# Two regions instead of three for the dense weights of a hybrid decoder trunk, and an early load of the third expert pair's down weights

## What is computed

```python
h = x @ w_in                                   # (256,1024) @ (1024,2048)
u, q, k, v, qm = jnp.split(h, list(SPLITS), axis=-1)
q, k = partial_rotary(heads(q), cos, sin), partial_rotary(heads(k), cos, sin)
y_pool = multiscale_pool(u, w_pool, pool_scale)
y_dsa = dilated_attention(q, k, heads(v))      # 8 heads x 64
km, vm = jnp.split(mem @ w_mem_kv, 2, axis=-1)
y_mem = memory_attention(heads(qm), heads(km), heads(vm))   # 4 heads x 64
mix = jnp.concatenate([y_pool, y_dsa, y_mem], axis=-1) @ w_out
x = layer_norm(DEEPNORM_ALPHA * x + mix, ln1_g, ln1_b)
# 64 routed experts of width 256, top 8 of them for each token, and one shared expert
top_idx, top_w = route(x, w_router, router_bias)
ffn = routed_experts(x, top_idx, top_w, w_gate, w_up, w_down) + swiglu(x, ws_gate, ws_up, ws_down)
x = layer_norm(DEEPNORM_ALPHA * x + ffn, ln2_g, ln2_b)
```

## Time and profile before

| | |
|---|---|
| median of 3 runs | 1214.82 us (1214.5 to 1215.64) |
| the profiled execution, by its own time | 1215.07 us |
| its span, first to last instruction | 1213.0 us |
| TensorE busy | 1180.3 us, 97% of the span |
| read from HBM | 450.15 MB |
| DMA over the span | 373 GB/s |
| dense part of layer 0, then its loop | up to 156.19 us, then to about 601 us |
| dense part of layer 1, then its loop | up to 752.81 us, then to 1199.5 us |

### The profile page before, as it was taken

One profiled execution on the slowest core, in us unless ns is written; L12 is line 12 of the kernel. 1 busy time (PEld: TensorE's weight loads), 2 busy tenths in 40 slices (PEclk: granted clock), 3 DMA queues, 4 the chain that ended last, 5 costly groups with the idle time before them and its releaser, 6 DMA issues.

```text
span 1213.0 us, 17943 instructions
## 1 busy us (share of the span) xinstructions
PE 1180.3 (97%) x7776; PEld 560.9 (46%) x7776; DVE 351.0 (29%) x1071; ACT 263.0 (22%) x513; POOL 10.4 (1%) x20
## 2 busy tenths in 40 slices
PE   7999999999999999999899999999999999999994
PEld 6774544444444444444386645444444444444431
DVE  0433722222222222222334246222222222222224
ACT  1132322112222122221112313222212222112210
POOL 0000000000000000000000000000000000000001
PEclk9999999999999999999999999999999999999998
DMA  9972399999999999999997406999999999999992
GB/s 385 424 317 73 119 408 427 429 425 427 428 425 428 427 427 428 427 426 426 421 388 306 182 35 242 405 427 427 427 426 428 426 427 428 427 427 427 427 426 111
DMA packets 36070, 452.45 MB, mean 373 GB/s; under 512 B 3984, under 2 KB 4112, under 8 KB 6928
## 3 DMA queue, kind: packets, MB, share of 16 engines
q1 hardware_dynamic: 35984, 451.22, 88.5%
HBM read 450.15 MB, written 1.05 MB: 372 GB/s over the span
## 4 chain that ended last, share of the span: by engine, by line
PE 90%; DMA 7%; DVE 2%; ACT 1%; issue 0%; POOL 0%; POOLq 0%; DVEq 0%
PE bank L620 34%; PE bank L646 17%; PE bank L540 8%; DMA slots<-in_w_gu 7%; PE bank L565 5%; PE bank L719 5%; PE bank L791 4%; PE bank L728 2%; PE bank L632 2%; PE bank L917 1%; PE bank L738 1%; PE bank L748 1%; PE bank L587 1%; PE bank L552 1%; PE bank L824 1%; PE bank L674 1%
## 5 line engine op out<-in xcount | busy, mean ns | idle before, releaser
L646 PE MATMUL bank<-slots,low 128*32 128x512 f32 x2048 | 233.0, 595 | 2.3 <-issue 2.3
L620 PE MATMUL bank<-slots,low 128*64 128x512 f32 x1024 | 226.9, 594 | 3.6 <-DMA slots<-in_w_gu 3.5
L620 PE MATMUL bank<-slots,xT 128*64 128x512 f32 x1024 | 226.3, 594 | 1.3 <-ACT xT L956 1.0
L1238 DVE SCALAR_TENSOR_TENSOR yparts<-bank,small,yparts 128x512 fp32r<-128x512 f32 x128 | 96.1, 751 | 249.1 <-ACT yparts L956 249.1
L540 PEld LDWEIGHTS bank<-high,low 128*128 128x128 bf16 x1536 | 108.2, 147 | 50.3 <-issue 49.7
L620 PEld LDWEIGHTS bank<-slots,low 128*64 128x64 f32 x1024 | 69.0, 137 | 134.3 <-issue 127.0
L620 PEld LDWEIGHTS bank<-slots,xT 128*64 128x64 f32 x1024 | 69.2, 137 | 131.1 <-issue 128.1
L1230 DVE TENSOR_TENSOR high<-high,bank 128x256 f32<-128x256 f32 x64 | 27.0, 421 | 329.7 <-ACT high L978 329.7
L956 ACT ACTIVATE yparts<-bank,small 128x512 fp32r<-128x512 f32 x128 | 88.1, 688 | 157.9 <-PE bank L646 157.9
L540 PE MATMUL bank<-high,low 128*128 128x128 bf16 x1536 | 117.7, 227 | 0.2
L646 PEld LDWEIGHTS bank<-slots,low 128*32 128x32 f32 x2048 | 60.7, 109 | 121.1 <-issue 117.2
(11 more groups left out here) (129 smaller groups left out, 667.4 us busy)
## 6 DMA issues: line engine op xcount, KB each, us to landing
slots<-in_w_gu SPq DMA_DIRECT2D x128, 2048.0 KB, 24.6
slots<-in_w_dn SPq DMA_DIRECT2D x64, 2048.0 KB, 24.4
slots<-in_dense SPq DMA_DIRECT2D x30, 1024.0 KB, 15.2
slots<-in_first SPq DMA_DIRECT2D x4, 768.0 KB, 7.7
r<-in_pool_mat SPq DMA_DIRECT2D x2, 1024.0 KB, 23.9
r<-in_ln_g SPq DMA_DIRECT2D x4, 512.0 KB, 4.8
r<-in_ln_b SPq DMA_DIRECT2D x4, 512.0 KB, 5.9
slots<-in_shared_dn SPq DMA_DIRECT2D x2, 1024.0 KB, 5.0
```

The costliest lines, as they stand in the source:

```text
L620: m = pe.matmul(H[64 * a:64 * a + 64, :], xg[B % 2][:, k, j, a, :], GU[g][:, a, :, k, :], start=k == 0, stop=k == KD - 1)
L646: m = pe.matmul(Y[half][r0:r0 + 32, :], hT[:, kc * P + 64 * a + 32 * t:kc * P + 64 * a + 32 * t + 32], DN[g][:, a, kc, half * 512:(half + ...
L1238: dve.scalar_tensor_tensor(ysp[:, 1, half * 512:(half + 1) * 512], Y[half][:, :], wslot[:, b:b + 1], ysp[:, 0, half * 512:(half + 1) * 512 ...
```

## The change

The dense blocks rotate through regions 0 and 1 alone: block c goes to region c % 2, and its load waits for the last use of block c - 2 rather than c - 3. Region 2, the DN of slot 2, is no longer used by dense weights, and the down weights of pair 2 are loaded into it early: in layer 0 behind pair 1's weights, in layer 1 at the head of the layer, once pair 29 has used its own. The GU of pair 2 is loaded in the other order: its second half (region 1) after sh1, its first half (region 0) after acc3. The small loads (tokens, router and small weights, pooling matrix) change their place in SyncE's order, and layer 0's pair 0 goes from ahead of them to behind blocks 3 and 4. Pair 1's weights stand behind block 5 as they did, but block 5 waited for raw3 and now waits for v1. `shared_up` of the first token tile waits for the two halves of its block apart.

```diff
--- before.py
+++ after.py
@@ -407,9 +407,9 @@
 
             def chunk(l, c):
 
-                r = c % 3
-                if c > 3 or c == 3 and l:
-                    sp.wait_ge(*full_at(l, LAST_USE[c - 3]))
+                r = c % 2
+                if c >= 3 or c == 2 and l:
+                    sp.wait_ge(*full_at(l, LAST_USE[c - 2]))
                 name = CHUNKS[c]
                 if name == "sd":
                     sp.dma_start(region[r][:, 0:KF * D], shared_dn[l]).then_inc(chunk_in[r][0], 16)
@@ -471,36 +471,42 @@
                 if l == 0:
                     sp.dma_start(cst[:], consts).then_inc(const_in, 16)
                     sp.dma_start(bo[:], before_ones).then_inc(const_in, 16)
+                    chunk(l, 2)
+                    sp.dma_start(xs[:], x[0].rearrange("(t p) d -> p t d", p=P)).then_inc(x_in, 16)
+                    sp.dma_start(sw[:], small_w[l]).then_inc(small_in, 16)
+                    sp.dma_start(r8[:], pool_mat).then_inc(pool_in, 16)
+                    chunk(l, 3)
+                    chunk(l, 4)
+                    load_gu(main, l, 0, 0)
+                    load_dn(main, l, 0, 0)
                 else:
                     sp.wait_ge(main.y_full, 2 * last + 2)
-                chunk(l, 2)
-                if l == 0:
+                    load_dn(main, l, 2, 2)
+                    sp.wait_ge(main.y_full, 2 * (l * PAIRS - 1))
+                    load_gu(main, l, 0, 0)
+                    load_dn(main, l, 0, 0)
+                    chunk(l, 2)
+                    sp.wait_ge(*x_before(l))
+                    sp.dma_start(sw[:], small_w[l]).then_inc(small_in, 16)
+                    sp.dma_start(r8[:], pool_mat).then_inc(pool_in, 16)
                     chunk(l, 3)
-                if l:
-                    sp.wait_ge(main.y_full, 2 * (l * PAIRS - 1))
-                load_gu(main, l, 0, 0)
-                load_dn(main, l, 0, 0)
-                if l == 0:
-                    sp.dma_start(xs[:], x[0].rearrange("(t p) d -> p t d", p=P)).then_inc(x_in, 16)
-                else:
-                    sp.wait_ge(*x_before(l))
-                sp.dma_start(sw[:], small_w[l]).then_inc(small_in, 16)
-                sp.dma_start(r8[:], pool_mat).then_inc(pool_in, 16)
-                for c in range(3 if l else 4, 6):
-                    chunk(l, c)
+                    chunk(l, 4)
+                chunk(l, 5)
                 load_gu(main, l, 1, 1)
                 load_dn(main, l, 1, 1)
+                if l == 0:
+                    load_dn(main, l, 2, 2)
                 chunk(l, 6)
-                chunk(l, 7)
                 sp.wait_ge(*full_at(l, "pooled"))
                 norms(l, ln1_g, ln1_b)
+                chunk(l, 7)
                 chunk(l, 8)
                 sp.wait_ge(*x_at(l, 0, NT - 1))
                 norms(l, ln2_g, ln2_b)
                 sp.wait_ge(*full_at(l, "sh1"))
-                load_gu(main, l, 2, 2)
+                load_gu(main, l, 2, 2, (1,))
                 sp.wait_ge(*full_at(l, "acc3"))
-                load_dn(main, l, 2, 2)
+                load_gu(main, l, 2, 2, (0,))
                 run(main, l, l, None)
                 with sp.If(count_in[sp.engine, l] > SLOTS):
                     rounds(sp, l, run)
@@ -529,7 +535,7 @@
             def chunk_wait(l, c, halves=(0, 1)):
 
                 for h in halves:
-                    pe.wait_ge(chunk_in[c % 3][h], 48 * l + 16 * (c // 3) + (16 if c % 3 else 0))
+                    pe.wait_ge(chunk_in[c % 2][h], 64 * l + 16 * (c // 2 + (c % 2 or l)))
 
             def gather(ps, B, quarter, buf, to=G):
 
@@ -580,7 +586,7 @@
                 pe.wait_ge(*read_at(l, f"shT{t}"))
                 if t == 0 and half == 1:
                     chunk_wait(l, 8)
-                wd = region[2][:, 0:KF * D].rearrange("p (k n) -> p k n", k=KF)
+                wd = region[0][:, 0:KF * D].rearrange("p (k n) -> p k n", k=KF)
                 name = f"acc{2 * t + half}"
                 o = fill(l, name)
                 for kc in range(KF):
@@ -716,7 +722,7 @@
                         for k in range(KD):
                             if i % 2 == 0 and j == 0 and k % 4 == 0:
                                 chunk_wait(l, c, (k // 4,))
-                            m = pe.matmul(o[:, j * S:(j + 1) * S], W[c][:, k, (2 * (i % 2) + j) * P:(2 * (i % 2) + j + 1) * P],
+                            m = pe.matmul(o[:, j * S:(j + 1) * S], W[c % 2][:, k, (2 * (i % 2) + j) * P:(2 * (i % 2) + j + 1) * P],
                                           xT[:, k, :], start=k == 0, stop=k == KD - 1)
                     filled(l, f"raw{i}", m)
 
@@ -725,7 +731,7 @@
                         chunk_wait(l, 3)
                     o = fill(l, f"v{t}")
                     for k in range(KD):
-                        m = pe.matmul(o[:, :], xT[:, k, t * P:(t + 1) * P], W[0][:, k, :],
+                        m = pe.matmul(o[:, :], xT[:, k, t * P:(t + 1) * P], W[1][:, k, :],
                                       start=k == 0, stop=k == KD - 1)
                     filled(l, f"v{t}", m)
 
@@ -735,7 +741,7 @@
                         fill(l, "u")
                     o = bank[BANK_OF["u"]]
                     for k in range(KD):
-                        m = pe.matmul(o[:, t * 256:(t + 1) * 256], xT[:, k, t * P:(t + 1) * P], W[1][:, k, 0:256],
+                        m = pe.matmul(o[:, t * 256:(t + 1) * 256], xT[:, k, t * P:(t + 1) * P], W[0][:, k, 0:256],
                                       start=k == 0, stop=k == KD - 1)
                     if t == NT - 1:
                         filled(l, "u", m)
@@ -745,7 +751,7 @@
                         fill(l, "qm")
                     o = bank[BANK_OF["qm"]]
                     for k in range(KD):
-                        m = pe.matmul(o[:, j * S:(j + 1) * S], W[1][:, k, 256 + j * P:256 + (j + 1) * P], xT[:, k, :],
+                        m = pe.matmul(o[:, j * S:(j + 1) * S], W[0][:, k, 256 + j * P:256 + (j + 1) * P], xT[:, k, :],
                                       start=k == 0, stop=k == KD - 1)
                     if j == 1:
                         filled(l, "qm", m)
@@ -778,7 +784,7 @@
                 def project(i, ks):
 
                     name, t, half = f"wo{i}", i // 2, i % 2
-                    w = W[2 if half == 0 else 0]
+                    w = W[1 if half == 0 else 0]
                     if not any(j == i for j, _ in begun):
                         chunk_wait(l, 5 + half)
                         fill(l, name)
@@ -914,6 +920,8 @@
                         fill(l, f"sh{t}")
                     o = bank[BANK_OF[f"sh{t}"]]
                     for k in ks:
+                        if t == 0 and k in (0, 4):
+                            chunk_wait(l, 7, (k // 4,))
                         m = pe.matmul(o[:, :], xT[:, k, t * P:(t + 1) * P], W[1][:, k, :],
                                       start=k == 0, stop=k == KD - 1)
                     if ks[-1] == KD - 1:
@@ -922,7 +930,6 @@
                 turn_tile(0)
                 project(3, [6, 7])
                 router(0)
-                chunk_wait(l, 7)
                 shared_up(0, [0, 1, 2, 3, 4, 5])
                 turn_tile(1)
                 shared_up(0, [6, 7])
```

## The result

| | median | runs | lowest to highest |
|---|---|---|---|
| before | 1215.10 us | 4 | 1214.5 to 1215.64 |
| after | 1222.28 us | 4 | 1221.25 to 1223.2 |

The ratio after to before is 1.006, 95% interval 1.0048 to 1.0073: the change makes the kernel 7.2 us slower. The forecast was 1217.9 us, with a range up to 1221.2. The profiled execution of the changed kernel took 1223.2 us by its own time and has a span of 1221.1 us, 8.1 more than before.

What follows compares the result with a forecast made beforehand. TensorE was taken to bound the kernel, with DMA nearly level in the loop and late at its end. Terms 5.9 + 1.8 - 4.6 = +3.1 on 1215.07 gave 1218.2, set to 1217.9 us for the median; range 1214.4 to 1221.2.

Steps and rivals of the forecast that it cites:

- The place and the mechanism of the stall: Layer 0, project(1): TensorE stands from 95.6 to 101.5 because wo1 queues behind pair 1 and pair 2's DN.
- Rival (b): Layer 0: wo1 is served beside the 8 MB, no stall, only the tail's gain stays: 1210.2 us; chance 0.06.
- Its size: TensorE's wait for wo1 in layer 0: +5.9 us, bounds 5.3 and 6.7.
- The clock: TensorE's clock falls inside the wo1 stall, with some microseconds at the lower level behind it: +1.8 us, bounds 0 and 3.6.
- Rival (a): At the wo1 wait the 5.9 us stall comes but the clock does not fall: 1216.1 us; chance 0.20.
- The gain at the ends of the loops: Pairs 29 to 31, both layers: pair 2's early DN removes TensorE's weight waits, -4.6 us, bounds -3.5 and -4.9.
- From there the DMA never runs dry: Layer 0's loop, after pair 3's DN lands at 176.9: each issue stands 7.2 us or more ahead of its landing.
- Rival (c): Loops: the stream is not ahead, as TensorE releases pair 3's load; the end waits stay: 1222.5 us; chance 0.08.
- The rest: sgu and sd cost 0, at worst 0.5 us a layer; k and wo1 of layer 1 do not stall.
- Rival (d): Layer 1: a further stall, of k or wo1, of one to three microseconds: 1219 to 1221 us; chance 0.10.

Runs made afterwards that it cites:

- the kernel with one early quarter: Kernel with pair 1 behind wo1, only pair 3's first GU half in two pieces, the first released 1.8 us earlier: 1211.42 us, ratio 0.9969 to the kernel before.

## Why the prediction was wrong

**The place and the mechanism of the stall: right.** One wait of TensorE for wo1 at the ninth instruction of the group, caused by the 8 MB that SyncE issues ahead of it. The experiments with the DN and pair 1 moved show it twice: 2 MB less, 2.5 us of wait; 8 MB less, none. Rival (b), wo1 served beside the others, is out: its first half lands at 101.2 with everything issued ahead of it landed by 98.8, and its second 2.5 us behind. What the Trainium skill says of completion out of order ("DMA: Bandwidth & Descriptors", section "Queues, rings and completion order") the large loads of this kernel did not show: all of them landed in the order of issue. Only the two kernels with loads in pieces throughout have cases of it, three in all, each by 0.3 to 0.4 us (a GU piece issued at 609.65 lands at 628.0, a DN half issued at 604.53 at 628.4).

**Its size: 7.3 us instead of 5.9, above the bound of 6.7.** TensorE came 1.0 us later to everything in that profile, which moves wait and landing alike and costs nothing here. The rest is wo0's second half, 1.2 us late against the working, and all behind it keeps that. The bound's reason ("a late DMA engine among the 16") named the right kind of thing and was too small. The DMA view of 75.5 to 79.2 us in the changed kernel has in it two fetches of instructions beside the loads:

```profile
q1 hardware_dynamic: 156, 1.59, 103.5%
q8 instruction: 1, 0.02, 1.8%
q14 instruction: 1, 0.01, 0.7%
```

Each lies on one DMA engine, the first for 1.06 us. A load ends on each of the 16 engines at a time of its own, and it has landed when the last is through. In the packets of this trace the engines end wo0's first half within 0.7 us of each other (74.5 to 75.2); its second half fourteen of them end by 77.7 and the last two at 78.4 and 78.7. Ten other kernels with wo0 in this place have 3.3 to 3.9 us between its halves and a fetch in the same stretch. In the eleventh, the one with every DN in halves, the fetch comes at 73.51, in the first half, and there it is the first half that is late, 3.9 us behind the load ahead of it, and the second follows at 2.4. In the kernel before a fetch of 1.09 us at 75.63 delays no landing (72.67, 77.56, 80.03: 4.9 and 2.5 us apart), but there the engines ended the load ahead already 3.2 us apart (69.0 to 72.2). The delay goes with the fetch, then; no run took the fetch away.

**The clock: right, 2.1 us for 1.8.** The fall inside the wait, the work at half pace and the return are in the windows, and the run with TensorE kept busy takes just this part away. Rival (a) is out. The rule of the Trainium skill ("TensorE: Matmul & The Clock Gate", section "HAM oscillation — how this bites in real kernels"), that a wait for DMA between bursts leaves the next burst cold, now has its number here, 2.1 us behind a wait of 7; by that rule, the trace agrees.

**The gain at the ends of the loops: wrong, -2.3 for -4.6 (bounds -3.5 and -4.9), and this is the step that failed.** The prediction set each load down 4.9 us behind the one ahead of it, said "From there the DMA never runs dry", and had "the stream is ahead by 2.6 us". Pair 3's DN, issued at 179.83 and landing 9.6 us later, is at 189.4; TensorE is 10.4 us later than before at that place, so the lead over the earlier trace rows (179.5) is 0.5 us. It should have been 7.5 us from issue to landing. In layer 1 the same reading (landings at 777.0 before and 785.6 after, TensorE 9.8 later) gives a lead of 1.2 us. The gains, 0.6 and 1.7, go with these leads. The landings at the head of layer 0's loop, GU of pair 2 (issued at 155.69 and 162.98), first GU half and DN of pair 3 (170.27 and 179.83):

```profile
slots<-in_w_gu SPq DMA_DIRECT2D x1, 2048.0 KB, 7.2
...
slots<-in_w_gu SPq DMA_DIRECT2D x1, 2048.0 KB, 8.5
...
slots<-in_w_gu SPq DMA_DIRECT2D x1, 2048.0 KB, 7.3
...
slots<-in_w_dn SPq DMA_DIRECT2D x1, 2048.0 KB, 9.6
```

And the DMA share (second last column) in the windows around them, in the changed kernel:

```profile
168.00:172.00 4.00, 4.00 (x22) 1.35 (x20) 0.00 (x0) 0.00 (x0) 0.00 (x0) 1.00 0.65 213
172.00:176.00 4.00, 3.82 (x34) 2.19 (x30) 0.85 (x2) 0.98 (x2) 0.00 (x0) 1.00 0.92 389
176.00:180.00 4.00, 4.00 (x42) 1.28 (x41) 0.75 (x1) 1.45 (x3) 0.00 (x0) 1.00 0.99 422
180.00:184.00 4.00, 4.00 (x20) 1.26 (x18) 1.48 (x6) 0.52 (x1) 0.00 (x0) 1.00 0.96 365
```

and in the kernel with the DN late, whose TensorE is 10.6 us earlier there, so that it is the same place of the loop:

```profile
168.00:172.00 4.00, 4.00 (x30) 1.25 (x24) 2.23 (x7) 0.97 (x2) 0.00 (x0) 1.00 1.01 434
```

The idle time ahead of pair 3's first half (0.65 in the first window) was in the working, and on TensorE's clock both GU halves of pair 3 landed where it has them: 167.2 and 172.1 for 167.1 and 172.0. The DN alone is 2.1 us late. The engines did not stand still for it: they are full in the windows (0.99 and 0.96), and yet move only 365 GB/s from 180 to 184. The packets show how: the 16 engines end the GU half within 0.5 us of each other (181.6 to 182.1) and go on with the DN at once, but most of its first packets take 0.7 to 1.3 us where 0.61 is usual, and one engine fetches instructions from 183.03 for 1.16 us. They end the DN between 186.8 and 188.9, the one with the fetch last, 0.5 us behind the next. It took 9.6 us, more than the 7.2 of a load on an idle queue.

Two things can add up to the 2.1 us, as other loads tell. One is a load that is issued just ahead of the landing in front of it, when the queue is nearly empty: this DN was issued 2.6 us ahead of it, and in the kernel with one early quarter a load issued at 164.42, 2.7 us ahead and with no fetch in it, lands 6.1 us behind the one in front, 1.2 late; pair 3's second half here, issued 3.9 us ahead, lands 4.9 behind. The other is the fetch: pair 2's second half met an idle queue, has a fetch in it at 168.97, and took 8.5 us for 7.2. The shares in this DN are not shown apart.

The late DN says how the 2.3 us are made up: the rotation costs 2.5 over both loops, the early DN is worth 4.9. The working had both, as 4.9 less 2.3 of idle time in each loop, so that is not a second error; the landing that it then took for sure is. Rival (c), no lead at all, was nearest to the time (1222.5 for 1222.28), and by luck: it denied the 2.3 us that were gained, and its stall and clock were 1.7 us too small.

**The rest: right.** Neither k nor wo1 nor sgu and sd waited in layer 1: behind wo1 of layer 0 the two timelines keep one distance, 10.4 us, to the end of the first loop, and behind that the next until pair 29 of the second. Rival (d) is out.

**Together:** +5.9 + 1.8 - 4.6 = +3.1 was forecast; in the profiles it is +7.3 + 2.1 - 2.3 = +7.1 beside the late start, and the medians have +7.2. Of the 4.0 us between the two, 2.3 are the gain at the ends, 1.4 the stall's size and 0.3 the clock.

## What to carry to other kernels

When a load is moved ahead on an in-order queue, list what is issued between it and the next load with a date, and add up bytes: the early load is paid by the one behind it. The same loads placed behind one block more kept the gain and lost the cost. A transfer lands with the slowest of its DMA engines, so a lead that is worked out from bytes alone is an upper bound: here two microseconds of it went in one load, which met a nearly empty queue and had a fetch of instructions beside it. Splitting a transfer to release it earlier seems to pay once, at the head of the stream, and costs in each further repetition.

## What the hardware showed that was not expected

A short gap can put the clock down. The kernel with pair 1 behind wo1 had in its profiled execution gaps of 1.02, 0.94 and 1.59 us at the end of the first loop, the last ahead of the last combine, and then, in these windows at the start of layer 1:

```profile
600.00:604.00 4.00, 3.21 (x13) 2.33 (x14) 2.70 (x5) 1.45 (x2) 0.00 (x0) 0.77 1.05 436
604.00:608.00 4.00, 4.00 (x16) 3.44 (x15) 3.93 (x8) 0.00 (x0) 1.36 (x3) 0.80 1.00 422
```

TensorE ran at 1.2 GHz for 3.4 us of these eight, and lost 1.7 us. That execution took 1215.37 us by its own time against a median of 1212.93; the second profile of the same kernel, with gaps of 1.24, 0.56 and 1.58 us there, has 1.00 in both windows and a span of 1211.1 us instead of 1213.4. A wait of 2.50 us (the DN behind wo1) did not move the clock in the execution profiled, one of 2.64 us (the kernel with every DN in halves, at 466 us) did. So with gaps of one to three microseconds the same program keeps its clock in one execution and not in another, and what decides is not shown. It is one part of the spread between runs and not all of it: the kernel before ran from 1214.01 to 1216.97 us with a mean clock of 0.995 or 0.996 each time.

The engines keep the distance that they have. In a full queue each of the 16 DMA engines takes 4.9 us for its part of 2 MB, and one that is late by a fetch stays late: in the kernel with the late DN one engine ends a load at 160.5 where the others end by 159.3, and the next three loads end with the same spread of 1.6 to 1.7 us. By 390 us the first and the last engine of the kernel before end a load 4.0 us apart.

Runs of 2 KB, with one more DMA for each pair, took the DMA engines from 425 to 409 GB/s at the same busy share. A further DMA of 1 MB in a full stream cost 0.1 us.
